# Expert stage of a hybrid encoder block: gate and up products issued as halves of both, and the next tile's rows turned in one place

## The chip, the core and the metric

The program runs on one core of a Trainium2 chip. The metric is the device time of one execution in microseconds (us). TensorE (PE in the profile) multiplies and turns, ScalarE (ACT) and VectorE (DVE) evict and split, GpSimd (POOL) gathers rows and adds results back with indirect DMAs, SyncE (SP) issues the weight loads.

## The reference, cut to what matters

The block projects 2048 tokens of width 1024, runs two attention mixers, merges them, and ends with a mixture of experts. Each token goes to 2 of 32 experts. The change touches this last part alone:

```python
order = jnp.argsort(eid)
tok = order // TOP_K
sizes = jnp.bincount(eid, length=N_EXPERTS).astype(jnp.int32)
xs = xt[tok]
hgu = lax.ragged_dot(xs, w_gate_up, sizes)
g, u = jnp.split(hgu, 2, axis=-1)
ys = lax.ragged_dot(jax.nn.silu(g) * u, w_down, sizes)
ys = ys * wts.reshape(-1)[order][:, None].astype(ys.dtype)
out = jnp.zeros((t, dm), ys.dtype).at[tok].add(ys)
```

`w_gate_up` is 32 x 1024 x 1024 (columns 0 to 511 gate, 512 to 1023 up), `w_down` is 32 x 512 x 1024, all float32.

## The kernel before, in words

Stages follow each other: projection, differential attention, window attention, merge and router, routing tables, experts (`expert_phase`, L2033 to L2340), final normalization. The change is in `expert_phase`.

**Precision.** Every float32 operand of a product is split into a rounded high part (ACT writes it as float32r) and the rest (DVE subtracts). A product is three matmuls: high x high, low x high, high x low. The stationary operand is the activation (128 x 128), the moving one the weight row slice.

**Tiles.** The routing stage sorts the tokens by expert and pads each expert to whole tiles of 128 tokens; `bounds` holds the first tile of each expert, which the engines read into registers (L2073 to L2077). For these inputs there are 49 tiles for 32 experts. PE runs a loop over experts and in it one over the expert's tiles (L2200 to L2217). ACT, DVE and POOL write out an expert's first tile and loop over its further ones.

**A tile on PE.** `gate_or_up` (L2168 to L2183) is called for gate with 512 columns into `p_gate` (8 slices k of the depth, 3 matmuls each, 24 in all), then for the two halves of up with 256 columns into `p_up0` and `p_up1` (24 matmuls each). In the middle of the second half of up, PE turns the first half of `h` (`turn_h(g, 0)`). Then it turns the first half of the next tile's gathered rows `xg` into `px` (`turn_x(g + 1, 0)`, 4 transposes of 128 columns, L2209), multiplies with `w_down` by 4 slices of the depth (`down`, 6 matmuls of 512 columns each, L2185 to L2195), turns the second half of `h` after the first slice (L2213) and the second half of the rows before the last (L2216). `px` has one bank of 512 columns, so the second half may be turned only when DVE has read the first (the wait on `x_lo`, L2155).

**A tile on ACT** (`tile`, L2237 to L2248): Silu of the 512 gate columns into `act_g`; in the first tile of an expert the high parts of slices 0 to 2 of the next expert's weights (`high`, L2221); the high part of the first half of the turned `h` (`hh`); slice 3; the second half of `hh`; the high part of the first half of the next rows (`high_x`, L2233). The second `high_x` follows in the next tile's or expert's code (L2255, L2274, L2279), and so does `result` (L2260), which evicts `py` times the token weights into `yo`.

**A tile on DVE** (`tile`, L2295 to L2317): waits for the Silu, multiplies `act_g` with each half of up as it comes (L2296 to L2298), and subtracts for the low parts of the next expert's early slices, of `h` (`low_h`, L2300) and of the rows (`low_x`, L2290).

**Weights.** An expert's 12 slices (8 of gate and up, 4 of down, 512 KB each) are loaded into `raw` by SP, each as soon as DVE has made the low part of the same slice for the expert before (L2090 to L2096). ACT and DVE make high and low parts: slices 0 to 3 have two places each, so they are made during the expert's first tile (`EARLY = 4`); slices 4 to 7 wait for the last tile's up products, slices 8 to 11 for its down products (L2225 to L2230).

**Rows.** POOL waits until both halves of a tile's rows are turned (L2122, L2128), gathers the next tile's rows, then waits for `yo` and adds the result of the tile before to `acc` (L2109 to L2117).

Of the kernel before, what the change touches and what calls it, by code (L numbers as in the profile page):

```python
# [21 lines left out]
P = 128  # L22
SEQ = 2048
D = 1024
# [2008 lines left out]
def expert_phase(nc, ident, x1, idx, weight, bounds, raw, load_raw, acc):  # L2033
# [6 lines left out]
    EARLY = 4  # L2040
    LATE_X = 6
    KF = FF // P
    NS = KD + KF
# [3 lines left out]
    with Phase(nc, "e") as ph:  # L2047
# [18 lines left out]
        picked, gathered, x_turned, x_hi, x_lo = (ph.sem(n) for n in ("picked", "gathered", "x_turned", "x_hi", "x_lo"))  # L2066
        gate_done, up_done, silu_done, h_done, h_turned, h_hi, h_lo = (
            ph.sem(n) for n in ("gate_done", "up_done", "silu_done", "h_done", "h_turned", "h_hi", "h_lo"))
        down_done, y_out, added, picked_out = ph.sem("down_done"), ph.sem("y_out"), ph.sem("added"), ph.sem("picked_out")
# [79 lines left out]
        def _(pe):  # L2149
            pe.sem_inc(up_done, 1)  # L2150
            pe.sem_inc(down_done, 1)

            def turn_x(g, half):

                pe.wait_ge(x_lo, 2 * g + half + 1)  # L2155
                for c in range(0, HX, P):
                    at = half * HX + c
                    last = nc.tensor.transpose(px[:, c:c + P], xg[:, at:at + P], ident[:])
                last.then_inc(x_turned, 1)
# [40 lines left out]
            with pe.Fori(0, NE) as e:  # L2200
                b0, b1 = tiles(pe, e)
                with pe.Fori(b0, b1) as g:

                    gate_or_up(g, e, p_gate, slice(0, FF), gate_done)
                    for p in range(PIECES):
                        gate_or_up(g, e, p_up[p], slice(FF + p * HP, FF + (p + 1) * HP), up_done)

                    pe.wait_ge(gathered, 16 * (g + 2))
                    turn_x(g + 1, 0)  # L2209

                    pe.wait_ge(y_out, g + 1)
                    down(g, e, 0)
                    turn_h(g, 1)  # L2213
                    down(g, e, 1)
                    down(g, e, 2)
                    turn_x(g + 1, 1)  # L2216
                    down(g, e, 3).then_inc(down_done, 1)  # L2217

        @block.scalar
        def _(act):  # L2220
            def high(e, b0, slices):  # L2221
                for s in slices:
                    if not (isinstance(e, int) and e == 0):
                        act.wait_ge(raw_in[s], 16 * e)
                    if s >= EARLY:  # L2225

                        if s < KD:
                            act.wait_ge(up_done, PIECES * b0 + 1)
                        else:
                            act.wait_ge(down_done, b0 + 1)  # L2230
                    nc.scalar.activation(wh[:, slot(e, s), :], raw[:, s:s + 1, :], ACT.Copy).then_inc(w_hi, 1)  # L2231

            def high_x(g, half):  # L2233
                act.wait_ge(x_turned, 2 * g + half + 1)
                nc.scalar.activation(xh[:, half * HX:(half + 1) * HX], px[:], ACT.Copy).then_inc(x_hi, 1)

            def tile(g, early_of=None):  # L2237
                act.wait_ge(gate_done, g + 1)
                nc.scalar.activation(act_g[:], p_gate[:], ACT.Silu).then_inc(silu_done, 1)
                if early_of is not None:  # L2240

                    high(early_of, None, range(EARLY - 1))
                for p in range(PIECES):
                    act.wait_ge(h_turned, PIECES * g + p + 1)
                    nc.scalar.activation(hh[:, piece(p)], phh[p][:, 0:HP], ACT.Copy).then_inc(h_hi, 1)
                    if early_of is not None and p == 0:
                        high(early_of, None, range(EARLY - 1, EARLY))
                high_x(g + 1, 0)  # L2248

            def expert(e, last):  # L2250
                b0, b1 = tiles(act, e)
                tile(b0, None if last else e + 1)
                with act.If(b0 + 1 < b1):
                    with act.Fori(b0 + 1, b1) as g:
                        high_x(g, 1)  # L2255
                        result(g - 1)
                        tile(g)
                return b1
# [12 lines left out]
            with act.Fori(0, NE - 1) as e:  # L2271
                b1 = expert(e, False)
                high(e + 1, b1, range(EARLY, LATE_X))
                high_x(b1, 1)  # L2274
                high(e + 1, b1, range(LATE_X, KD))
                result(b1 - 1)
                high(e + 1, b1, range(KD, NS))
            b1 = expert(NE - 1, True)
            high_x(b1, 1)  # L2279
            result(b1 - 1)  # L2280

        @block.vector
        def _(dve):
            dve.sem_inc(x_lo, 1)

# [4 lines left out]
            def low_x(g, half):  # L2290
                dve.wait_ge(x_hi, 2 * g + half + 1)
                at = slice(half * HX, (half + 1) * HX)
                nc.vector.tensor_tensor(xl[:, at], px[:], f(xh[:, at]), ALU.subtract).then_inc(x_lo, 1)

            def tile(g, early_of=None):  # L2295
                def multiply(p):  # L2296
                    dve.wait_ge(up_done, PIECES * g + p + 2)
                    nc.vector.tensor_tensor(h[:, piece(p)], act_g[:, piece(p)], p_up[p][:, 0:HP], ALU.mult).then_inc(h_done, 1)  # L2298

# [8 lines left out]

                dve.wait_ge(silu_done, g + 1)
                multiply(0)  # L2310
                early(0, 1)
                low_h(0)
                multiply(1)
                early(2)
                low_h(1)
                low_x(g + 1, 0)
                early(3)  # L2317

            def expert(e, last):
                b0, b1 = tiles(dve, e)  # L2320
                tile(b0, None if last else e + 1)
                with dve.If(b0 + 1 < b1):
                    with dve.Fori(b0 + 1, b1) as g:
                        low_x(g, 1)
                        tile(g)
# [7 lines left out]
            with dve.Fori(0, NE - 1) as e:  # L2333
                b1 = expert(e, False)
                for s in range(EARLY, NS):
                    if s == LATE_X:
                        low_x(b1, 1)
                    low(e + 1, s)
            b1 = expert(NE - 1, True)
            low_x(b1, 1)  # L2340

# [163 lines left out]
```

## Time and profile before

| | |
|---|---|
| median of 3 runs | 2822.14 us (2819.76 to 2827.99) |
| the profiled execution | 2831.76 us |
| its span, first to last instruction | 2830.0 us |
| mean granted TensorE clock over the span | 0.955 of full |
| PE busy | 2608.0 us (92%) |
| DVE busy | 1625.0 us (57%) |
| ACT busy | 1190.8 us (42%) |
| experts stage, first gate matmul to the last tile's down products | about 1859.7 to 2758 us |

All stretches and starts below are us from the span's start. A busy figure of PE counts overlapping matmuls once; matmuls are pipelined, so the distance from one start to the next tells what a matmul costs in a stream, not its recorded duration. "issue" as a releaser means that the profile shows nothing the engine waited for. Names carry a stage's letter: `e_px` is `px` of the expert stage, `rw_raw` is `raw`.

### The profile page before, as it was taken

Reading aid. Unit: us, or ns where it says so; the run is one execution under the profiler, and the core shown is the slowest. Engines: PE = TensorE matmul, PEld = TensorE weight load, DVE = VectorE, ACT = ScalarE, POOL = GpSimd, SP = SyncE. Lnnn points to the kernel's source line nnn. Section 1 sums busy time; section 2 is a strip of 40 time slices with the busy share of each in tenths; the row PEclk is TensorE's granted clock in tenths of the full one; section 3 lists DMA queues with packets and bytes.
Section 4 is the critical chain, followed back from the end, with each engine's and each line's share of the span. In section 5 each row is a group of like instructions: output and inputs, shape, how many; then the busy total and the mean of one; then the engine's idle time right before and its main releaser. Section 6 shows DMA issues by size and latency. Waiting matters only on the chain. (4 is left out here: it accounts for less than half of the span.)

```text
span 2830.0 us, 45509 instructions
## 1 busy us (share of the span) xinstructions
PE 2608.0 (92%) x14631; PEld 2248.3 (79%) x14632; DVE 1625.0 (57%) x3059; ACT 1190.8 (42%) x2016; POOL 527.2 (19%) x538
## 2 busy tenths in 40 slices
PE   6999996899999999989799999589999999999990
PEld 5888885788888888889688888378888888888880
DVE  6323332666666666559544443667585577557846
ACT  3111111445444454447211111357585567556746
POOL 0111111101001010035233332012222222222220
PEclk9999998999999999969899999789999999999995
DMA  6344444756575564279433443469787788768946
GB/s 227 121 158 135 143 153 139 226 183 205 166 213 172 190 208 145 102 178 230 156 117 130 134 139 136 149 209 377 235 316 244 229 294 307 235 227 316 381 123 260
DMA packets 261732, 566.40 MB, mean 200 GB/s; under 512 B 27025, under 2 KB 119953, under 8 KB 259585
## 3 DMA queue, kind: packets, MB, share of 16 engines
q1 hardware_dynamic: 170192, 430.50, 44.6%
q0 software_dynamic: 18720, 64.96, 8.8%
q10 hardware_dynamic: 72720, 69.68, 7.4%
q8 instruction: 56, 0.92, 0.1%
q14 instruction: 44, 0.35, 0.0%
HBM read 433.45 MB, written 131.60 MB: 200 GB/s over the span
## 5 line engine op out<-in xcount | busy, mean ns | idle before, releaser
L2288 DVE TENSOR_TENSOR e_wl<-rw_raw,e_wh 128x1024 fp32r<-128x1024 f32 (+1 forms) x384 | 449.4, 1220 | 18.2 <-ACT e_wh L2231 13.8
L2231 ACT ACTIVATE e_wh<-rw_raw 128x1024 fp32r<-128x1024 f32 (+1 forms) x384 | 380.6, 1054 | 6.4 <-PEq L76 6.4
L246 PE MATMUL j_pg<-qkv_w_hi,j_xh 128*128 128x512 f32 (+1 forms) x640 | 243.6, 381 | 9.2 <-DVE qkv_w_lo L416 9.2
L248 PE MATMUL j_pg<-qkv_w_lo,j_xh 128*128 128x512 f32 (+1 forms) x640 | 238.0, 372 | 0.0
L247 PE MATMUL j_pg<-qkv_w_hi,j_xl 128*128 128x512 f32 (+1 forms) x640 | 237.3, 371 | 0.0
L2180 PE MATMUL e_p_up<-e_wh,e_xh 128*128 128x256 f32 (+1 forms) x784 | 225.5, 288 | 0.0
L2182 PE MATMUL e_p_up<-e_wl,e_xh 128*128 128x256 f32 (+1 forms) x784 | 221.7, 283 | 0.0
L2181 PE MATMUL e_p_up<-e_wh,e_xl 128*128 128x256 f32 (+1 forms) x784 | 221.7, 283 | 0.0
L1136 PE MATMUL b_pg<-b_g_wh,b_g_xh 128*128 128x512 f32 x512 | 209.0, 408 | 0.7 <-DVE b_g_out L1323 0.7
L1193 ACT ACTIVATE b_th<-b_t 128x512 fp32r<-128x512 f32 (+3 forms) x160 | 85.4, 534 | 285.6 <-PE b_t L1121 276.8
L1136 PE MATMUL b_pg<-b_g_wl,b_g_xh 128*128 128x512 f32 x512 | 204.8, 400 | 0.0
L1136 PE MATMUL b_pg<-b_g_wh,b_g_xl 128*128 128x512 f32 x512 | 203.5, 397 | 0.0
L1267 DVE TENSOR_SCALAR_CACHE_REDUCE b_sc<-b_s 128x512 f32<-128x512 f32 (+3 forms) x320 | 179.2, 605 | 30.4 <-PE b_s L1108 18.6
L2192 PE MATMUL e_py<-e_wh,e_hh 128*128 128x512 f32 x392 | 166.8, 425 | 0.4
L1308 DVE TENSOR_TENSOR b_tl<-b_t,b_th 128x512 fp32r<-128x512 f32 (+3 forms) x160 | 97.6, 610 | 119.8 <-ACT b_th L1193 119.8
L445 DVE TENSOR_TENSOR j_by_cos<-j_pg,qkv_cos 128x512 f32<-128x512 f32 x64 | 37.7, 589 | 216.4 <-DMA v_lo<-j_staged 145.8
L2180 PE MATMUL e_p_gate<-e_wh,e_xh 128*128 (+1 forms) x392 | 156.8, 400 | 1.3 <-issue 1.3
L1186 ACT ACTIVATE b_sc<-b_sc,b_nb 128x128 f32<-128x128 f32 (+15 forms) x128 | 153.1, 1197 | 6.8 <-DVE b_nb L1278 6.8
L2194 PE MATMUL e_py<-e_wl,e_hh 128*128 128x512 f32 x392 | 154.5, 394 | 0.0
L2193 PE MATMUL e_py<-e_wh,e_hl 128*128 128x512 f32 x392 | 153.6, 392 | 0.0
L2182 PE MATMUL e_p_gate<-e_wl,e_xh 128*128 (+1 forms) x392 | 153.4, 391 | 0.0
L2181 PE MATMUL e_p_gate<-e_wh,e_xl 128*128 (+1 forms) x392 | 153.4, 391 | 0.0
(350 smaller groups left out, 6634.8 us busy)
## 6 DMA issues: line engine op xcount, KB each, us to landing
rw_raw<-w_gate_up SPq DMA_DIRECT2D x256, 512.0 KB, 7.3
rw_raw<-w_down SPq DMA_DIRECT2D x128, 512.0 KB, 9.5
b_g_xh<-xt_hi SPq DMA_DIRECT2D x64, 512.0 KB
b_g_xl<-xt_lo SPq DMA_DIRECT2D x64, 512.0 KB
gates<-b_g_out ACTq DMA_DIRECT2D x64, 256.0 KB, 5.2
m_gt<-gates SPq DMA_DIRECT2D x16, 1024.0 KB, 8.3
qk_hi<-j_staged ACTq DMA_DIRECT2D x16, 832.0 KB, 4.5
qk_lo<-j_staged ACTq DMA_DIRECT2D x16, 832.0 KB, 6.9
```

Of the source, the lines that this page charges most:

```text
L246: nc.tensor.matmul(out, xh[:, u, ks], w_hi[:, k, cs], start=(k == 0), stop=False)
L247: nc.tensor.matmul(out, xl[:, u, ks], w_hi[:, k, cs], start=False, stop=False)
L248: last = nc.tensor.matmul(out, xh[:, u, ks], w_lo[:, k, cs], start=False, stop=(k == KD - 1))
L1136: last = nc.tensor.matmul(pg[:], x_side, w_side, start=(q == 0), stop=(q == PASSES - 1))
L1267: nc.vector.tensor_scalar(sc[u][:, m, ks], bank[n % 4][:, 0:ks.stop - ks.start], 1.0, NEG, ALU.mult, ALU.max, accum_out=mx[:, u, m, g:g + ...
L2180: nc.tensor.matmul(out[:, 0:js.stop - js.start], xh[:, at], hi, start=(k == 0), stop=False)
L2181: nc.tensor.matmul(out[:, 0:js.stop - js.start], xl[:, at], hi, start=False, stop=False)
L2182: last = nc.tensor.matmul(out[:, 0:js.stop - js.start], xh[:, at], lo, start=False, stop=(k == KD - 1))
L2192: nc.tensor.matmul(py[:, js], hh[:, at], wh[:, n, js], start=(k == 0), stop=False)
L2194: last = nc.tensor.matmul(py[:, js], hh[:, at], wl[:, n, js], start=False, stop=(k == KF - 1))
L2231: nc.scalar.activation(wh[:, slot(e, s), :], raw[:, s:s + 1, :], ACT.Copy).then_inc(w_hi, 1)
L2288: nc.vector.tensor_tensor(wl[:, slot(e, s), :], raw[:, s:s + 1, :], f(wh[:, slot(e, s), :]), ALU.subtract).then_inc(w_lo, 1)
```

## The change

- Gate and up are no longer separate products. Piece p (of two) is columns 256 p to 256 p + 255 of gate and the same of up: one matmul of 512 columns, whose moving operand is two runs of 256 columns that lie 512 apart in the weight slice. Piece p goes to its own bank `p_gu[p]`, gate in its first half and up in its second. 48 matmuls of 512 columns take the place of 24 of 512 and 48 of 256.
- `turn_h(g, 0)` stands before slice 6 of the second piece (before: before slice 4 of the second half of up).
- Silu is done by halves of 256 columns, one after each piece; the second stands behind the early slice 3 on ACT. DVE multiplies a half as soon as its Silu is done.
- `px` has two banks. Both halves of the next rows are turned together, ahead of the down products; ACT's two `high_x` stand before the second half of `hh`, DVE's two `low_x` before the second `low_h`. The places in the next tile's and the next expert's code are gone. The first slice of the first piece waits for the first half of the rows, slice 4 for the second.
- On DVE, early slice 2 comes before the second multiplication.

```diff
+    TURN_AT = 3 * KD // 4
...
-        p_gate, p_up = ph.ps("p_gate", [P, FF]), [ph.ps(f"p_up{p}", [P, BANK]) for p in range(PIECES)]
-        py, px = ph.ps("py", [P, D]), ph.ps("px", [P, HX])
+        p_gu = [ph.ps(f"p_gu{p}", [P, 2, HP]) for p in range(PIECES)]
+        py, px = ph.ps("py", [P, D]), ph.ps("px", [P, D])
...
-            def gate_or_up(g, e, out, js, done):
+            def gate_and_up(g, e, p):
+
                 for k in range(KD):
-                    if out is p_gate:
+                    if p == 0:
                         if k % (KD // 2) == 0:
 
-                            pe.wait_ge(x_lo, 2 * g + 2 + 2 * k // KD)
+                            pe.wait_ge(x_lo, 2 * g + 3 + 2 * k // KD)
                         wait_low(pe, e, k)
-                    if out is p_up[1] and k == KD // 2:
+                    elif k == TURN_AT:
 
                         turn_h(g, 0)
                     at = slice(k * P, (k + 1) * P)
-                    hi, lo = wh[:, slot(e, k), js], wl[:, slot(e, k), js]
-                    nc.tensor.matmul(out[:, 0:js.stop - js.start], xh[:, at], hi, start=(k == 0), stop=False)
-                    nc.tensor.matmul(out[:, 0:js.stop - js.start], xl[:, at], hi, start=False, stop=False)
-                    last = nc.tensor.matmul(out[:, 0:js.stop - js.start], xh[:, at], lo, start=False, stop=(k == KD - 1))
-                last.then_inc(done, 1)
+                    hi, lo = (w[:, slot(e, k), :].rearrange("p a (b n) -> p (a b) n", b=2)[:, :, piece(p)] for w in (wh, wl))
+                    nc.tensor.matmul(p_gu[p][:], xh[:, at], hi, start=(k == 0), stop=False)
+                    nc.tensor.matmul(p_gu[p][:], xl[:, at], hi, start=False, stop=False)
+                    last = nc.tensor.matmul(p_gu[p][:], xh[:, at], lo, start=False, stop=(k == KD - 1))
+                last.then_inc(gu_done, 1)
...
-                    gate_or_up(g, e, p_gate, slice(0, FF), gate_done)
                     for p in range(PIECES):
-                        gate_or_up(g, e, p_up[p], slice(FF + p * HP, FF + (p + 1) * HP), up_done)
+                        gate_and_up(g, e, p)
 
                     pe.wait_ge(gathered, 16 * (g + 2))
                     turn_x(g + 1, 0)
+                    turn_x(g + 1, 1)
 
                     pe.wait_ge(y_out, g + 1)
                     down(g, e, 0)
                     turn_h(g, 1)
                     down(g, e, 1)
                     down(g, e, 2)
-                    turn_x(g + 1, 1)
                     down(g, e, 3).then_inc(down_done, 1)
...
             def tile(g, early_of=None):
-                act.wait_ge(gate_done, g + 1)
-                nc.scalar.activation(act_g[:], p_gate[:], ACT.Silu).then_inc(silu_done, 1)
-                if early_of is not None:
-
-                    high(early_of, None, range(EARLY - 1))
-                for p in range(PIECES):
+                def silu(p):
+                    act.wait_ge(gu_done, PIECES * g + p + 2)
+                    nc.scalar.activation(act_g[:, piece(p)], p_gu[p][:, 0, :], ACT.Silu).then_inc(silu_done, 1)
+
+                def high_h(p):
                     act.wait_ge(h_turned, PIECES * g + p + 1)
                     nc.scalar.activation(hh[:, piece(p)], phh[p][:, 0:HP], ACT.Copy).then_inc(h_hi, 1)
-                    if early_of is not None and p == 0:
-                        high(early_of, None, range(EARLY - 1, EARLY))
+
+                def early(*slices):
+                    if early_of is not None:
+                        high(early_of, None, slices)
+
+                silu(0)
+                early(0, 1, 2)
+                high_h(0)
+                early(3)
+                silu(1)
                 high_x(g + 1, 0)
+                high_x(g + 1, 1)
+                high_h(1)
...
-            dve.sem_inc(x_lo, 1)
+            dve.sem_inc(x_lo, 2)
...
             def tile(g, early_of=None):
                 def multiply(p):
-                    dve.wait_ge(up_done, PIECES * g + p + 2)
-                    nc.vector.tensor_tensor(h[:, piece(p)], act_g[:, piece(p)], p_up[p][:, 0:HP], ALU.mult).then_inc(h_done, 1)
+                    dve.wait_ge(silu_done, PIECES * g + p + 1)
+                    nc.vector.tensor_tensor(h[:, piece(p)], act_g[:, piece(p)], p_gu[p][:, 1, :], ALU.mult).then_inc(h_done, 1)
...
-                dve.wait_ge(silu_done, g + 1)
                 multiply(0)
                 early(0, 1)
                 low_h(0)
+                early(2)
                 multiply(1)
-                early(2)
+                low_x(g + 1, 0)
+                low_x(g + 1, 1)
                 low_h(1)
-                low_x(g + 1, 0)
                 early(3)
```

## Rows read from the trace of the kernel before

**Rows 1.** Groups of instructions of 1800 to 2830, counts and mean ns of one

```profile
L2239 ACT ACTIVATE e_act_g<-e_p_gate 128x512 f32<-128x512 f32 x49 | 29.4, 599 | 72.2 <-PE e_p_gate L2182 71.8
```

**Rows 2.** Busy time by stretch: PE, PEld, DVE, ACT, POOL, then PEclk, DMA share, GB/s

```profile
1859.00:2750.00 891.00, 889.87 (x5247) 776.05 (x5248) 575.82 (x668) 563.05 (x699) 198.09 (x193) 1.00 0.80 274
...
2099.58:2117.99 18.41, 18.41 (x109) 15.94 (x109) 16.50 (x19) 15.99 (x20) 4.30 (x4) 1.00 1.03 385
...
2136.42:2154.49 18.07, 18.07 (x110) 15.79 (x108) 5.07 (x9) 6.08 (x9) 3.63 (x4) 1.00 0.51 170
```

**Rows 3.** Waits of 1855 to 2750: us in total, times, longest

```profile
PEld e_py L2192 <- issue: 7.1, 30, 0.3
```

**Rows 4.** Timeline of PE, an expert's first tile: start, us, what

```profile
2099.58 0.50 PE L2180 MATMUL e_p_gate<-e_wh,e_xh 128*128 x1
...
2105.13 0.28 PE L2180 MATMUL e_p_up<-e_wh,e_xh 128*128 x1
...
2109.44 0.38 PE L2165 MATMUL e_phh<-ident,e_h 128*128 128x128 f32 x2
2109.58 0.36 PE L2180 MATMUL e_p_up<-e_wh,e_xh 128*128 128x256 f32 x1
...
2111.10 0.60 PE L2158 MATMUL e_px<-ident,e_xg 128*128 128x128 f32 x4
2111.70 0.49 PE L2192 MATMUL e_py<-e_wh,e_hh 128*128 128x512 f32 x1
...
2113.18 0.38 PE L2165 MATMUL e_phh<-ident,e_h 128*128 128x128 f32 x2
2113.32 0.48 PE L2192 MATMUL e_py<-e_wh,e_hh 128*128 128x512 f32 x1
...
2116.16 0.60 PE L2158 MATMUL e_px<-ident,e_xg 128*128 128x128 f32 x4
2116.52 0.48 PE L2192 MATMUL e_py<-e_wh,e_hh 128*128 128x512 f32 x1
```

**Rows 5.** Timeline of PE in an expert's second tile, which starts at 2136.42

```profile
2147.84 0.60 PE L2158 MATMUL e_px<-ident,e_xg 128*128 128x128 f32 x4
2148.20 0.48 PE L2192 MATMUL e_py<-e_wh,e_hh 128*128 128x512 f32 x1
```

**Rows 6.** Timeline of ACT in the tile of rows 4

```profile
2105.68 1.28 ACT L2239 ACT_TABLE_LOAD   x1
2106.98 0.60 ACT L2239 ACTIVATE e_act_g<-e_p_gate 128x512 f32<-128x512 f32 x1
2107.47 2.94 ACT L2231 ACTIVATE e_wh<-rw_raw 128x1024 f32 x3
2110.32 0.37 ACT L2245 ACTIVATE e_hh<-e_phh 128x256 fp32r<-128x256 f32 x1
2110.58 1.06 ACT L2231 ACTIVATE e_wh<-rw_raw 128x1024 f32 x1
2113.60 0.39 ACT L2245 ACTIVATE e_hh<-e_phh 128x256 fp32r<-128x256 f32 x1 [1.97 <-PE e_phh L2165]
```

**Rows 7.** Timeline of DVE in the tile of rows 4

```profile
2108.20 0.42 DVE L2298 TENSOR_TENSOR e_h<-e_act_g,e_p_up 128x256 f32<-128x256 f32 x1 [0.61 <-PE e_p_up L2182]
...
2111.05 0.42 DVE L2302 TENSOR_TENSOR e_hl<-e_phh,e_hh 128x256 fp32r<-128x256 f32 x1
...
2114.02 0.42 DVE L2302 TENSOR_TENSOR e_hl<-e_phh,e_hh 128x256 fp32r<-128x256 f32 x1 [1.09 <-ACT e_hh L2245]
2114.51 0.69 DVE L2293 TENSOR_TENSOR e_xl<-e_px,e_xh 128x512 fp32r<-128x512 f32 x1
```

**Rows 8.** Landing of weight loads issued in 2062.74 to 2081.17, then 2117.99 to 2136.42

```profile
DMA to landing us min/median/max: 7.5/9.5/9.8
...
DMA to landing us min/median/max: 11.2/11.4/11.6
```

**Rows 9.** Timeline of PE ahead of the first tile

```profile
1857.36 1.11 PE L2158 MATMUL e_px<-ident,e_xg 128*128 128x128 f32 x4 [1.41 <-DVE e_xl L2293]
```

More of the change, by code:

```diff
@@ L2066, in expert_phase @@
         picked, gathered, x_turned, x_hi, x_lo = (ph.sem(n) for n in ("picked", "gathered", "x_turned", "x_hi", "x_lo"))
-        gate_done, up_done, silu_done, h_done, h_turned, h_hi, h_lo = (
-            ph.sem(n) for n in ("gate_done", "up_done", "silu_done", "h_done", "h_turned", "h_hi", "h_lo"))
+        gu_done, silu_done, h_done, h_turned, h_hi, h_lo = (
+            ph.sem(n) for n in ("gu_done", "silu_done", "h_done", "h_turned", "h_hi", "h_lo"))
         down_done, y_out, added, picked_out = ph.sem("down_done"), ph.sem("y_out"), ph.sem("added"), ph.sem("picked_out")
@@ L2149, in _ @@
         def _(pe):
-            pe.sem_inc(up_done, 1)
+            pe.sem_inc(gu_done, 1)
             pe.sem_inc(down_done, 1)
@@ L2155, in turn_x @@
                 pe.wait_ge(x_lo, 2 * g + half + 1)
-                for c in range(0, HX, P):
-                    at = half * HX + c
-                    last = nc.tensor.transpose(px[:, c:c + P], xg[:, at:at + P], ident[:])
+                for at in range(half * HX, (half + 1) * HX, P):
+                    last = nc.tensor.transpose(px[:, at:at + P], xg[:, at:at + P], ident[:])
                 last.then_inc(x_turned, 1)
@@ L2227, in high @@
                         if s < KD:
-                            act.wait_ge(up_done, PIECES * b0 + 1)
+                            act.wait_ge(gu_done, PIECES * b0 + 1)
                         else:
@@ L2234, in high_x @@
                 act.wait_ge(x_turned, 2 * g + half + 1)
-                nc.scalar.activation(xh[:, half * HX:(half + 1) * HX], px[:], ACT.Copy).then_inc(x_hi, 1)
+                nc.scalar.activation(xh[:, half * HX:(half + 1) * HX], px[:, half * HX:(half + 1) * HX], ACT.Copy).then_inc(x_hi, 1)
             def tile(g, early_of=None):
-                act.wait_ge(gate_done, g + 1)
-                nc.scalar.activation(act_g[:], p_gate[:], ACT.Silu).then_inc(silu_done, 1)
-                if early_of is not None:
-                    high(early_of, None, range(EARLY - 1))
-                for p in range(PIECES):
+                def silu(p):
+                    act.wait_ge(gu_done, PIECES * g + p + 2)
+                    nc.scalar.activation(act_g[:, piece(p)], p_gu[p][:, 0, :], ACT.Silu).then_inc(silu_done, 1)
+                def high_h(p):
                     act.wait_ge(h_turned, PIECES * g + p + 1)
                     nc.scalar.activation(hh[:, piece(p)], phh[p][:, 0:HP], ACT.Copy).then_inc(h_hi, 1)
-                    if early_of is not None and p == 0:
-                        high(early_of, None, range(EARLY - 1, EARLY))
+                def early(*slices):
[6 more added lines that the diff above has]
+                silu(1)
                 high_x(g + 1, 0)
+                high_x(g + 1, 1)
+                high_h(1)
             def expert(e, last):
@@ L2254, in expert @@
                     with act.Fori(b0 + 1, b1) as g:
-                        high_x(g, 1)
                         result(g - 1)
@@ L2272, in _ @@
                 b1 = expert(e, False)
-                high(e + 1, b1, range(EARLY, LATE_X))
-                high_x(b1, 1)
-                high(e + 1, b1, range(LATE_X, KD))
+                high(e + 1, b1, range(EARLY, KD))
                 result(b1 - 1)
@@ L2278, in _ @@
             b1 = expert(NE - 1, True)
-            high_x(b1, 1)
             result(b1 - 1)
@@ L2292, in low_x @@
                 at = slice(half * HX, (half + 1) * HX)
-                nc.vector.tensor_tensor(xl[:, at], px[:], f(xh[:, at]), ALU.subtract).then_inc(x_lo, 1)
+                nc.vector.tensor_tensor(xl[:, at], px[:, at], f(xh[:, at]), ALU.subtract).then_inc(x_lo, 1)
             def tile(g, early_of=None):
                 def multiply(p):
-                    dve.wait_ge(up_done, PIECES * g + p + 2)
-                    nc.vector.tensor_tensor(h[:, piece(p)], act_g[:, piece(p)], p_up[p][:, 0:HP], ALU.mult).then_inc(h_done, 1)
+                    dve.wait_ge(silu_done, PIECES * g + p + 1)
+                    nc.vector.tensor_tensor(h[:, piece(p)], act_g[:, piece(p)], p_gu[p][:, 1, :], ALU.mult).then_inc(h_done, 1)
                 def low_h(p):
@@ L2323, in expert @@
                     with dve.Fori(b0 + 1, b1) as g:
-                        low_x(g, 1)
                         tile(g)
@@ L2335, in _ @@
                 for s in range(EARLY, NS):
-                    if s == LATE_X:
-                        low_x(b1, 1)
                     low(e + 1, s)
-            b1 = expert(NE - 1, True)
-            low_x(b1, 1)
+            expert(NE - 1, True)
 def final_phase(nc, acc, ln_g, ln_b, out):
```

## Prediction, made before the changed kernel was built or run

> **What bounds the kernel now.** I read the busy time by stretch first, with one stretch for the whole stage: PE is busy 889.87 of 891 us at full granted clock (1.00, the 2.4 GHz level), DVE 575.82, ACT 563.05 [rows 2]. The stage is TensorE's. Then the waits: the only one on PE that repeats is before the first `down` product, 7.1 us in 30 times [rows 3]. Then PE's timeline, tile by tile. There are 49 tiles [rows 1] of two kinds. An expert's further tiles take 18.07 us, an expert's first tile 18.41 [rows 2], and the difference sits mostly in one place: from the first turn of the rows to the first `down` product it is 0.60 us in a first tile [rows 4] and 0.36 in a further one [rows 5]. The wait's releaser is called issue, so I look for it on DVE: `low_h(0)` runs from 2111.05 for 0.42, to 2111.47, and PE goes on at 2111.70 [rows 4, 7]. The product waits for the low part of the first half of `h`, 0.24 us a time; 30 x 0.24 = 7.2 agrees with the 7.1. It is late since DVE could multiply only at 2108.20, when the first half of up was done, and then had two early slices to subtract.
>
> **Part 1, fewer matmuls for the same columns.** 36 matmuls of 256 columns take 2109.44 - 2105.13 = 4.31 us, 0.1197 each. For 512 columns I take two stretches of `down`: 6 matmuls behind four turns take 2113.18 - 2111.70 = 1.48, 12 behind two turns 2116.16 - 2113.32 = 2.84; the 6 more cost 1.36, 0.2267 each, and restarting behind turns costs 1.48 - 1.36 = 0.12 [rows 4]. Two of 256 columns cost 0.2394, one of 512 0.2267: 0.0127 less. A tile has 24 such pairs, so it gains 0.305 us. Restarting behind `turn_h(0)` goes from 0.08 (12 matmuls in 2111.10 - 2109.58 = 1.52, against 12 x 0.1197 = 1.44) to 0.12: 0.04 lost.
>
> No matmul of the trace has a moving operand in two runs, so its cost is bounded from both sides: 0.2267 as for one run of 512 (below nothing is excluded, since the same columns must be streamed), and 2 x 0.1197 = 0.2394 if each run costs what a matmul of its own does. I take 0.2267: 512 columns in one instruction is the nearer row, and a run is 1 KB long.
>
> What a matmul costs beyond its columns is 2 x 0.1197 - 0.2267 = 0.0127 us by the rows. The Trainium skill (TensorE: Matmul & The Clock Gate, the wait-not-56-ns section of Part 1 and Back-to-back issue gap) has a warm matmul cost its columns at 2.4 GHz plus about 2.5 ns. By that the pairs would give 24 x 2.5 ns = 0.06 us a tile in place of 0.31. The trace disagrees with it for these float32r streams; the sum goes by the rows.
>
> **Part 2, the rows turned in one place.** Four turns take 0.36, two 0.14 [rows 4, 5], so two more cost 0.22 and eight about 0.80. Before: 0.36 + 0.36 and a second restart of 0.12; after: 0.80. Gain 0.04, which cancels the loss of part 1. Their waits are long met: `px` halves are read in the tile before. POOL's gather starts some 4 us earlier in the tile, behind the earlier turns; it queues ahead of the same `add_rows` and its bytes are the same, and PE asks for them a tile later. `y_out` comes at the tile's start and is asked for 12 us into it.
>
> So each tile loses 0.305 us: 49 x 0.305 = **15.0 us**.
>
> **Part 3, the wait of first tiles.** After the change (offsets from the tile's start; before in brackets): first piece done 5.55 (2105.13 - 2099.58). On ACT the table load is at 6.10, Silu of 256 columns at 7.40 taking 0.37 as `hh` does (0.60), three slices from about 7.7 (7.89), `hh(0)` from 10.5 to 10.9 (10.74) [rows 6]. DVE multiplies behind the Silu and its own backlog at 8.1 (8.62); the two low slices end near 11.0, and `low_h(0)`, which before ran 11.47 to 11.89, ends at 11.4. PE needs it at 5.55 + (24 x 0.2267 + 0.14 + 0.12) + 0.80 = 12.05, later than its end plus the 0.23 it takes to release PE [rows 4, 7]. The wait goes: **7.1 us** [rows 3].
>
> What is late next is the chain behind the second piece, now longer by a Silu. The piece is done at 11.25; ACT is held by slice 3 (10.8 to 11.8), so Silu(1) runs to 12.2, DVE ends slice 2 about 12.6 and multiplies until 13.05. PE turns that half behind the first `down` slice, at 12.05 + 1.48 = 13.53: 0.3 to spare after the release. `hh(1)` comes 0.42 behind that turn and `low_h(1)` another 0.42 + 0.42 later, as at 2113.18, 2113.60, 2114.02 [rows 4, 6, 7]; so 14.79, plus 0.23 for the release 15.02, and PE asks for it at 13.53 + 0.14 + 1.48 = 15.15. The two `high_x` (12.2 to 13.3) and `low_x` (13.1 to 14.4, two of 0.69) [rows 7] fit between, but with little left: 0.1 us.
>
> **The rest.** The second Silu adds about 0.25 us of ACT, the added waits on ACT hold only copies that are not yet due, and ACT and DVE have 2 us of idle in an 18.41 us tile (15.99 and 16.50 busy) [rows 2]: nothing, for as long as that slack lasts. Ahead of the first tile the second half of the rows waits 1.41 us for `low_x` [rows 9]; with two banks it does not. Bounds 0 and 1.4 (the engine runs at half clock there, recorded at 1.11 for four turns, and part of what is gained early is spent at that clock); I take **1.0**.
>
> **Sum.** 15.0 + 7.1 + 1.0 = 23.1 us. The profiled execution took 2831.76 and would take 2808.7. It stands 9.6 above the median of the runs, 2822.14, so the median becomes **2799 us** (-0.8%). A first tile would take 18.41 - 0.305 - 0.24 = 17.87, a further one 17.76.
>
> **Rivals.**
> - *The wait stays, or moves* to `turn_h(1)` or to the third `down` slice, whose margins are 0.1 to 0.3 us. About 0.24 in each of 30 first tiles, 7.1 us: 2806. For: the thin margins; against: the work before them ends earlier in every step.
> - *A matmul's fixed cost is small*, so the merge gives back little. As a mechanism here, the surplus of the 256-column streams would have to lie elsewhere than in the instruction. 24 x 0.0025 x 49 = 2.9 in place of 15.0: 2811. Against: the two cadences of rows 4. This is the page's rule above.
> - *A run costs like a matmul* (the other bound): 48 x 0.0127 x 49 = 29.9 more: 2829. The gate columns, one run before, become two. For: no row excludes it; against: nothing is nearer to it than the plain 512 rows.
> - *The weight loads become the bound*, the rival on the slower side with a point of decision. In experts of one tile the 16 DMA engines show a share of 1.03 [rows 2], and from the first to the last of four such experts the median landing grows from 9.5 to 11.4 us [rows 8]: 0.63 an expert, so an expert's loads need about 18.41 + 0.63 = 19.05 us. At 17.87 it grows by 1.2, to 9.5 + 3 x 1.2 = 13.1. It decides once landing passes about 15 us, what is left of a tile when ACT must have slice 0 again (about 2.7 lie between its read and the next load). Four in a row is the longest I find, and an expert's further tiles (share 0.51) empty the queue. Were all 31 experts ahead of the last bound to 19.05: 31 x 1.18 = 37 us: 2836.
>
> **Numbers.** A measurement of this kernel tells about 0.3% (8.5 us) from no change. Forecast 0.66, wait stays 0.13, small fixed cost 0.06, run cost 0.07, loads 0.05, something between these that leaves it within 0.3% 0.03. Faster takes the first two and most of the third (2811 lies 11 below): 0.83; same: 0.05; slower: the run cost and the loads, 0.12. Range: 2790 (the median itself moved by 8 us over three runs, and the first-tile wait could leave more behind it than 0.24) to 2812, which takes in the wait and the small fixed cost; 0.15 is left out above.
>
> **What would show it.** PE's starts in the two pieces 0.227 apart (0.239: run cost); no gate or up stream of 0.12; tiles 17.87 and 17.76 apart; no wait row on `e_py`, or one on the third slice; the landing of weight loads at 12 to 13 us at the end of four experts, and no wait of `e_wh` on `rw_raw`; the granted clock at 1.00. I am wrong if the cadence is not 0.227, or if first tiles stay more than 0.2 us above further ones.

## Result and profile after

The changed kernel took 2802.35 us in the median of 6 runs (2796.89 to 2809.25), the kernel before in the same session 2827.88 (2819.76 to 2836.09); the ratio is 0.9915, with a 95% interval of 0.9899 to 0.9931. That is 24 us less, 20 to 29 by the interval; the forecast was 23.1 us less. 2802 lies in the range given. The profiled execution took 2799.30 (before: 2831.76). That is 32.5 less, and not all of it is the change's, as the account of the sum below shows.

The stage by stretch, from the first matmul of the second tile to that of the last (47 tiles; the very first tile runs in part at half clock, and its length varies by a microsecond from execution to execution). Columns as in [rows 2], where PEld is TensorE's loading of stationary operands; the second and the third line are a first tile and a further one:

```profile
1872.98:2706.99 834.01, 834.01 (x3949) 690.35 (x3948) 551.24 (x645) 559.24 (x723) 163.42 (x188) 1.00 0.83 284
2085.91:2103.64 17.73, 17.73 (x85) 14.69 (x85) 16.55 (x19) 16.41 (x21) 3.78 (x4) 1.00 1.03 384
2121.36:2139.09 17.73, 17.73 (x85) 14.69 (x84) 5.55 (x9) 7.30 (x11) 2.97 (x4) 1.00 0.71 235
```

The same stretch of the kernel before:

```profile
1879.90:2739.81 859.91, 859.52 (x5078) 749.27 (x5076) 553.02 (x645) 543.16 (x675) 192.54 (x188) 1.00 0.80 275
```

859.91 to 834.01: 25.9 us from 47 tiles. A first tile and a further one are now equally long, where they were 18.41 and 18.07 [rows 2]. PE's granted clock is 1.00 in both.

PE in that first tile (start, us, what). It answers to [rows 4]:

```profile
2085.91 0.39 PE L2181 MATMUL e_p_gu<-e_wh,e_xh 128*128 x1
2086.14 0.39 PE L2182 MATMUL e_p_gu<-e_wh,e_xl 128*128 x1
...
2095.43 0.39 PE L2165 MATMUL e_phh<-ident,e_h 128*128 128x128 f32 x2
2095.58 0.48 PE L2181 MATMUL e_p_gu<-e_wh,e_xh 128*128 128x512 f32 x1
...
2097.03 1.03 PE L2158 MATMUL e_px<-ident,e_xg 128*128 128x128 f32 x8
2097.82 0.48 PE L2193 MATMUL e_py<-e_wh,e_hh 128*128 128x512 f32 x1
...
2099.29 0.38 PE L2165 MATMUL e_phh<-ident,e_h 128*128 128x128 f32 x2
2099.42 0.48 PE L2193 MATMUL e_py<-e_wh,e_hh 128*128 128x512 f32 x1
...
2100.90 0.39 PE L2193 MATMUL e_py<-e_wh,e_hh 128*128 128x512 f32 x1
```

42 matmuls whose moving operand is two runs take 2095.43 - 2085.91 = 9.52 us, 0.2267 each: what one run of 512 columns costs in `down`. Eight turns take 0.79. And the wait before `down` [rows 3] is gone. The waits of PE's weight loads of 1850 to 2740, whole:

```profile
PEld e_px L2158 <- DMA e_xg<-x,e_idx_in: 7.5, 1, 7.5
PEld e_p_gu L2181 <- issue: 1.9, 1, 1.9
```

Both stand ahead of the first tile. A second wait, which is not in [rows 3], went too. In the kernel before, the weight loads that open an expert idled some 0.26 us in each of 31 tiles, and the stream there restarts 0.1 us late: the first 24 products take 5.55 us in [rows 4], and 5.44 in the changed kernel (2085.91 to 2091.35). These are 31 of the 32 times of this line of the kernel before (1855 to 2750):

```profile
PEld e_p_gate L2180 <- issue: 9.7, 32, 1.7
```

ACT and DVE in the tile of 2085.91 (answers to [rows 6, 7]):

```profile
2091.31 1.28 ACT L2240 ACT_TABLE_LOAD   x1
2092.61 0.39 ACT L2240 ACTIVATE e_act_g<-e_p_gu 128x256 f32<-128x256 f32 x1
2092.89 2.95 ACT L2231 ACTIVATE e_wh<-rw_raw 128x1024 f32 x3
2095.86 0.39 ACT L2244 ACTIVATE e_hh<-e_phh 128x256 fp32r<-128x256 f32 x1
...
2099.70 0.38 ACT L2244 ACTIVATE e_hh<-e_phh 128x256 fp32r<-128x256 f32 x1 [0.95 <-PE e_phh L2165]
```

```profile
2093.34 0.42 DVE L2303 TENSOR_TENSOR e_h<-e_act_g,e_p_gu 128x256 f32<-128x256 f32 x1 [0.22 <-issue]
2094.18 2.36 DVE L2293 TENSOR_TENSOR e_wl<-rw_raw,e_wh 128x1024 f32 x2 [0.42 <-ACT e_wh L2231]
2096.46 0.42 DVE L2307 TENSOR_TENSOR e_hl<-e_phh,e_hh 128x256 fp32r<-128x256 f32 x1
...
2097.93 0.41 DVE L2303 TENSOR_TENSOR e_h<-e_act_g,e_p_gu 128x256 f32<-128x256 f32 x1
2098.30 1.29 DVE L2298 TENSOR_TENSOR e_xl<-e_px,e_xh 128x512 fp32r<-128x512 f32 x2
2100.12 0.43 DVE L2307 TENSOR_TENSOR e_hl<-e_phh,e_hh 128x256 fp32r<-128x256 f32 x1 [0.54 <-issue]
```

The table load is at 5.40 us of the tile (2091.31 - 2085.91), 0.70 earlier than in [rows 6]; the first `low_h` ends at 10.97, and PE asks for it at 11.91.

### The profile page after: what moved, and what is told of

Read it like the earlier page. It is cut to its first block and busy times, and to the rows that moved or that the text cites. A ratio compares the mean times of both kernels' runs of the same rounds, so it can differ in the third digit from the quotient of the medians.

```text
span 2797.6 us, 42799 instructions
## 1 busy us (share of the span) xinstructions
PE 2576.8 (92%) x13455; PEld 2181.4 (78%) x13456; DVE 1622.0 (58%) x3059; ACT 1206.8 (43%) x2065; POOL 496.4 (18%) x538
## 5 line engine op out<-in xcount | busy, mean ns | idle before, releaser
L2181 PE MATMUL e_p_gu<-e_wh,e_xh 128*128 128x512 f32 (+1 forms) x784 | 310.4, 396 | 1.5 <-DVE e_xl L2298 1.5
L2183 PE MATMUL e_p_gu<-e_wl,e_xh 128*128 128x512 f32 (+1 forms) x784 | 306.2, 391 | 0.0
L2182 PE MATMUL e_p_gu<-e_wh,e_xl 128*128 128x512 f32 (+1 forms) x784 | 305.6, 390 | 0.0
L246 PE MATMUL j_pg<-qkv_w_hi,j_xh 128*128 128x512 f32 (+1 forms) x640 | 243.3, 380 | 10.1 <-DVE qkv_w_lo L416 10.1
L2181 PEld LDWEIGHTS e_p_gu<-e_wh,e_xh 128*128 128x128 f32 x784 | 147.6, 188 | 31.7 <-issue 1.9
L2183 PEld LDWEIGHTS e_p_gu<-e_wl,e_xh 128*128 128x128 f32 x784 | 147.4, 188 | 31.2
L2182 PEld LDWEIGHTS e_p_gu<-e_wh,e_xl 128*128 128x128 f32 x784 | 147.8, 188 | 28.3
L2193 PE MATMUL e_py<-e_wh,e_hh 128*128 128x512 f32 x392 | 161.1, 411 | 0.0
```

The lines of the kernel that those rows point to most:

```text
L246: nc.tensor.matmul(out, xh[:, u, ks], w_hi[:, k, cs], start=(k == 0), stop=False)
L2181: nc.tensor.matmul(p_gu[p][:], xh[:, at], hi, start=(k == 0), stop=False)
L2182: nc.tensor.matmul(p_gu[p][:], xl[:, at], hi, start=False, stop=False)
L2183: last = nc.tensor.matmul(p_gu[p][:], xh[:, at], lo, start=False, stop=(k == KD - 1))
L2193: nc.tensor.matmul(py[:, js], hh[:, at], wh[:, n, js], start=(k == 0), stop=False)
```

## The experiments

All ratios are to the kernel before. Each run's "steady" figure is the stretch of 47 tiles as above, of its one profiled execution: 859.91 before, 834.01 changed.

### What a matmul costs beyond its columns

`pairs_split`: each product of the changed kernel as two of 256 columns.

```diff
-                for k in range(KD):
+                for b, k in [(b, k) for b in range(2) for k in range(KD)]:
...
-                    nc.tensor.matmul(p_gu[p][:], xh[:, at], hi, start=(k == 0), stop=False)
+                    nc.tensor.matmul(p_gu[p][:, b, :], xh[:, at], hi[:, b, :], start=(k == 0), stop=False)
```

> The changed kernel with each product of 512 columns issued as two of 256 (the gate halves of all slices, then the up halves), into the same bank, with all else as in the changed kernel: 96 matmuls of 256 columns a tile for 48 of 512. Theory (each instruction costs 0.0127 us beyond its columns): starts 0.120 apart, 48 x 0.0127 = 0.61 us a tile more, less 0.04 for the cheaper restart behind the turns, 28 us in all, so it gives back the whole gain: ratio to the kernel before about 1.001, tiles about 18.3 us apart. Rival (a matmul costs some 2.5 ns beyond its columns, and the 256-column streams were slow for another reason): 6 us more than the changed kernel, ratio about 0.993.

Measured: ratio 1.0015 (1.0001 to 1.0029). The stretch:

```profile
1870.87:2736.22 865.35, 865.35 (x6206) 812.81 (x6205) 554.90 (x645) 559.20 (x723) 163.39 (x188) 1.00 0.81 273
```

865.35 - 834.01 = 31.3 us; further tiles are 18.33 long, 0.60 more than the 17.73 of the changed kernel, where 0.57 was expected. All of the gain is given back and a little more, since a tile now issues 96 products for gate and up where the kernel before issues 72. 3 us are a wait that the order of this experiment makes: its first sweep passes the 8 slices in 2.9 us and meets slices whose low part is not made yet (weight-load waits in the same stretch):

```profile
PEld e_p_gu L2181 <- DVE e_wl L2293: 2.9, 16, 0.2
```

So the cost is one of the instruction (0.60 / 48 = 0.0125 us each), and not of the gate, of the up or of a run. Each matmul here has a weight load of its own, and both were doubled; which of the two it is that costs, no run separates. The 2.5 ns that the Trainium skill gives for a warm matmul beyond its columns (TensorE: Matmul & The Clock Gate, Back-to-back issue gap) is not what these streams show.

### Which part ends the wait of first tiles

`merge_only`: merged products with the Silu in halves, but rows turned in two places through one bank. An excerpt of its edit against the changed kernel; ACT's and DVE's places for the rows go back with it:

```diff
-        py, px = ph.ps("py", [P, D]), ph.ps("px", [P, D])
+        py, px = ph.ps("py", [P, D]), ph.ps("px", [P, HX])
...
                     turn_x(g + 1, 0)
-                    turn_x(g + 1, 1)
...
                     down(g, e, 2)
+                    turn_x(g + 1, 1)
```

> The merged products alone: rows turned in two places through one bank, as before the change. Theory: the merge gives 0.27 us in each of 49 tiles (13 us), and it is the earlier multiplication that ends the wait of first tiles before the down products (7 us): the low part is ready at 11.2 us of the tile, PE asks at 11.5. Ratio about 0.993; no wait row on e_py. Rival (the wait went because eight turns now stand ahead of the down products): the wait of 0.24 us stays in 30 tiles, ratio about 0.995. Beside this, the matmul that opens a new expert restarted late by 0.10 us before the change and does not after it; if the late turning of the rows is why, 0.10 us in 31 tiles comes back here (first tiles 17.87, further ones 17.77), if not, both kinds are 17.77.

`rows_apart`: the same places, but with two banks.

> The changed kernel with the second turning of the rows, and what ACT and DVE do with them, put back where they were, but with two banks, so that the turning waits for nothing. Theory: the place of the turns is worth 0.04 us a tile for the merged restart and 0.10 us in each of 31 tiles that open an expert: 2 + 3 = 5 us more than the changed kernel, ratio about 0.993, same as the merge alone. Rival (the late start of an expert comes of the wait of the second turning for the low part of the first half, not of its place): first tiles as short as further ones, only 2 us more than the changed kernel, and faster than the merge alone.

Measured: 0.9954 (0.9939 to 0.9970) and 0.9954 (0.9936 to 0.9973), steady 849.22 and 849.15. The theory of `merge_only` was wrong on the wait, and that of `rows_apart` did not reckon with it: it stays in both. Weight-load waits from 1870 to 2740, of the first:

```profile
PEld e_py L2194 <- issue: 8.7, 30, 0.3
PEld e_p_gu L2182 <- issue: 8.0, 31, 0.3
```

and of the second:

```profile
PEld e_py L2193 <- issue: 12.1, 30, 0.4
```

First tiles are 18.22 long in both, further ones 17.77 to 17.82. The merge alone gives what its step said in further tiles (0.27), and in first tiles no more than 0.2. The late start of an expert is gone with two banks although the turns are late, as the rival of `rows_apart` said: it came with the second turning's wait for the low part of the first half, not with its place. (PE comes to the turns of a first tile at 11.15 us of it, in `merge_only` at 11.26. Why a wait that was met a microsecond before holds up the next expert, no view shows.) But the 0.1 us that this gave in each expert went into the other wait, which grew from 0.3 to 0.4: something else sets the length of a first tile.

What that is, ACT's timeline in `merge_only` shows, in the first tile that starts at 2082.23:

```profile
2081.03 0.60 ACT L2236 ACTIVATE e_xh<-e_px 128x512 fp32r<-128x512 f32 x1 [0.45 <-PE e_px L2159]
2081.52 2.00 ACT L2232 ACTIVATE e_wh<-rw_raw 128x1024 fp32r<-128x1024 f32 x2
2083.41 1.11 ACT L2273 ACTIVATE e_yo<-e_py,weight 128x1024 f32<-128x1024 f32 x1
2084.41 3.90 ACT L2232 ACTIVATE e_wh<-rw_raw 128x1024 fp32r<-128x1024 f32 x4
2088.33 1.28 ACT L2241 ACT_TABLE_LOAD   x1
2089.62 0.38 ACT L2241 ACTIVATE e_act_g<-e_p_gu 128x256 f32<-128x256 f32 x1
2089.90 2.94 ACT L2232 ACTIVATE e_wh<-rw_raw 128x1024 f32 x3
2092.75 0.37 ACT L2245 ACTIVATE e_hh<-e_phh 128x256 fp32r<-128x256 f32 x1
```

From the second turning of the rows to the high part of `h` there is no pause. The chain starts when PE has turned the second half, 1.2 us ahead of the tile, and ends 12 us later with the high part that DVE needs for the value PE waits for. Slices 6 and 7 in it wait only for the last tile's products with gate and up, which were done long before; they stand behind the turning for no reason of their own. From this came the next run.

`slices_first`: `rows_apart` with one exchange on ACT.

```diff
-                high(e + 1, b1, range(EARLY, LATE_X))
-                high_x(b1, 1)
-                high(e + 1, b1, range(LATE_X, KD))
+                high(e + 1, b1, range(EARLY, KD))
+                high_x(b1, 1)
                 result(b1 - 1)
```

> The kernel with the second turning put back (two banks), and one exchange on ACT: slices 6 and 7 of the next expert go ahead of the second high_x, which waits for that turning. Theory: the wait of first tiles before the down products is ACT's: from the second turning to the high part of h it runs without a pause (slices 6 and 7, the eviction of the result, slices 8 to 11, the table load, Silu, slices 0 to 2), and a late second turning holds it up by about a microsecond. With the exchange, the wait of 0.4 us in 30 tiles goes although the rows are still turned late: first tiles 17.8, ratio about 0.991, as of the changed kernel. Rival (the wait is the place of eight turns ahead of the down products, PE's own time): unchanged, first tiles 18.2, ratio 0.995.

Measured: 0.9917 (0.9898 to 0.9935), as good as the changed kernel. The stretch, and PE's waits of 1870 to 2740 whole:

```profile
1871.36:2707.49 836.13, 836.01 (x3949) 688.49 (x3948) 547.97 (x644) 548.00 (x722) 172.85 (x188) 1.00 0.82 283
```

```profile
PEld e_py L2193 <- issue: 0.4, 1, 0.4
```

The theory holds. 849.15 - 836.13 = 13.0 us come from the exchange alone. And 836.13 - 834.01 = 2.1 us, 0.045 a tile, is what turning the rows in one place is worth once the wait is gone: the restart of part 2 (0.04).

### Is it ACT in the kernel before, too?

`low_h_sooner`: the kernel before with an exchange on DVE (the edit below). `before_slices_first`: the kernel before with the exchange on ACT, as in `slices_first`.

```diff
-                early(0, 1)
+                early(0)
                 low_h(0)
+                early(1)
                 multiply(1)
```

> The kernel before with one exchange on DVE: the low part of the first half of h ahead of early slice 1. It prices the wait before the down products by itself. Theory: the high part is ready at 11.1 us of a first tile, the low part then ends at 11.6 in place of 11.9, and PE, which asks at 11.9, no longer waits: 30 x 0.24 = 7 us less, ratio 0.9975, first tiles 18.17. Rival: the wait moves on to the second turning of h or to the third down slice, since slices 1 and 2 now stand ahead of the second multiplication in other order: ratio 1.000.

> The kernel before, with the exchange on ACT alone (slices 6 and 7 ahead of the second high_x). Theory: before the merge it is the first multiplication, held until the first half of up is done at 8.4 us of the tile, that sets when DVE gets through two low slices to the low part of h (11.47); ACT earlier by a microsecond changes nothing there. The wait of 0.24 us stays in 30 tiles, ratio 1.000 within 0.0015. Rival (ACT's unbroken chain sets the wait in this kernel too): the wait goes, 7 us, ratio 0.997 or less.

Measured: 0.9966 (0.9952 to 0.9980) and 0.9969 (0.9957 to 0.9980); steady 852.00 and 853.08, so 7.9 and 6.8 us from a wait of 7.1. Either exchange ends it. The second theory was wrong: in this kernel, too, the wait goes when ACT comes earlier. In the kernel before, ACT stands for the second turning and then works without a pause until the table load of [rows 6]; the start of that chain, 1.2 us ahead of the tile of 2099.58:

```profile
2098.38 0.60 ACT L2235 ACTIVATE e_xh<-e_px 128x512 fp32r<-128x512 f32 x1 [0.43 <-PE e_px L2158]
```

DVE shows how this reaches PE. In `before_slices_first`, multiplication and next early slice:

```profile
2093.86 0.42 DVE L2297 TENSOR_TENSOR e_h<-e_act_g,e_p_up 128x256 f32<-128x256 f32 x1 [0.36 <-PE e_p_up L2182]
2094.20 1.22 DVE L2287 TENSOR_TENSOR e_wl<-rw_raw,e_wh 128x1024 f32 x1
```

and in the kernel before (the multiplication at 2108.20 stands in [rows 7]):

```profile
2108.77 1.23 DVE L2288 TENSOR_TENSOR e_wl<-rw_raw,e_wh 128x1024 f32 x1
```

0.34 from start to start against 0.57. The slice came 0.23 us late since ACT made its high part only from 2107.47 to 2108.52, and this is as much as the 0.24 that PE waited. The view prints no idle time there. The other half of what the prediction said stands: the multiplication at 2108.20 did wait 0.61 us for the first half of up [rows 7], and with one slice in place of two behind it the wait goes as well.

### An order that moves the wait

`merge_low_h_sooner`: `merge_only` with `low_h(0)` ahead of early slice 1, but slices 1 and 2 both ahead of the second multiplication. `merge_low_h_then`: the same with slice 2 behind it; DVE's edit of this one, against the changed kernel:

```diff
-                early(0, 1)
+                early(0)
                 low_h(0)
-                early(2)
+                early(1)
                 multiply(1)
+                early(2)
```

> The merged products alone, rows turned in two places, with the exchange on DVE: the low part of the first half of h ahead of early slice 1. Theory: in the merge alone the wait (0.28 us in 30 tiles) has the low part behind two early slices, of which slice 0 waits for ACT; with one slice in front it starts when ACT has the high part, at 10.9 us, ends at 11.3, and PE, which asks at 11.6, does not wait: 8 us less than the merge alone, ratio about 0.992, first tiles 17.9. Rival (the wait is ACT's high part itself): it shortens by less than half, ratio over 0.994.

> The merged products alone with the low part of the first half of h after one early slice, and slice 2 moved behind the second multiplication. The run before this one left two slices ahead of that multiplication behind the low part: DVE came to it at 13.5 us of the tile and PE waited 1.17 us at the second turning of h in 31 tiles. Theory: now the multiplication runs at 12.4, done at 12.8, and PE turns at 13.06 without a wait, so neither wait is left: first tiles 17.9, ratio about 0.992, against 0.9954 of the merge alone. Rival (DVE has too little room for either order, and some wait stays): ratio over 0.994.

Measured: 1.0028 (1.0016 to 1.0041), slower than the kernel before, and 0.9933 (0.9907 to 0.9958). Steady: 869.11 and 840.10. In the first the wait on `e_py` is gone as expected and another, four times as long, has come (waits of 1870 to 2740):

```profile
PEld e_phh L2166 <- DVE e_h L2307: 35.5, 30, 1.2
```

Two slices of 1.13 us ahead of the multiplication start it at 13.53 us of the tile, and PE wants to turn its result at about 13.1. In the second both waits are gone: first tiles 17.91, as expected (the late start of experts stays). One exchange of 1.1 us on an engine with 2 us of idle a tile is worth 29 us (869.11 - 840.10).

### The room of the second chain

`low_h_late`: the changed kernel with `early(3)` ahead of `low_h(1)` on DVE.

> The changed kernel with early slice 3 on DVE ahead of the low part of the second half of h. The prediction gave that chain 0.1 us to spare in a first tile. Theory: slice 3 takes DVE from about 14.1 to 15.3 us of the tile, the low part then comes at 15.7 in place of 14.65, PE asks for it at 15.0, so a wait of about 0.95 us appears on e_py in 30 to 31 first tiles: 29 us, first tiles 18.7, ratio about 1.002. Rival (the chain has more room than the arithmetic says, or the lost time is made good because the tile after starts with ACT and DVE further ahead): under 0.5 us a tile, ratio under 0.997.

Measured: 0.9957 (0.9941 to 0.9974), steady 847.36: 13.4 us more, 0.44 on average in each of 30 first tiles (18.11 to 18.37 long), where 0.95 was expected. The waits of 1867 to 2740, whole:

```profile
PEld e_py L2193 <- DVE e_wl L2293: 17.7, 30, 0.8
PEld e_p_gu L2181 <- issue: 2.9, 16, 0.2
```

The rival's number came, not by its reasons. The expectation let slice 3 start at 14.1; in the changed kernel DVE is through with the rows at 13.7 (2098.30 + 1.29 - 2085.91) and idle for 0.54 until 14.2, so the slice delays the low part by 1.13 - 0.54 = 0.59. The 0.1 us to spare that the prediction gave this chain was right: in the changed kernel the low part ends at 14.64, reaches PE 0.23 later at 14.87, and PE starts the third slice of the depth at 14.99 (2100.90). 0.59 less these 0.12 is 0.47 a tile, against the 0.44 measured.

### The weight loads

`loads_fewer`: it leaves out the loads of `w_down` after the first expert, so that its output is not the reference's; all instructions of PE, ACT and DVE stay. `loads_more`: one more load of 512 KB an expert. The edit of the first, on SP:

```diff
-                for s in range(NS):
+                for s in range(KD):
```

> The changed kernel without the loads of w_down after the first expert (its slices are split again for every expert, from the first expert's data): 8 loads of 512 KB for 12. Theory (loads are hidden at any landing under about 15 us): no difference from the changed kernel, ratio 0.9915 within 0.0015, tiles 17.73 to 17.78, DMA share about 0.75 in experts of one tile. Rival (the saturated DMA engines already cost something, in waits on the gathered rows or in slower access to the memories): 3 us or more faster than the changed kernel.

> The changed kernel with one more load of 512 KB an expert, into a buffer that nobody reads. At 384 GB/s an expert of one tile then needs (7.34 + 0.52) MB / 384 GB/s = 20.5 us of the DMA engines for 17.74 us of PE; the landing grows by 2.7 us an expert, from 6 to about 14 at the end of four, still inside 15. Theory: no difference from the changed kernel by more than 2 us in all. Rival (the loads are at their limit): every expert of one tile is lengthened towards 20.5 us, up to 2.7 us in each of some 14 tiles, and waits on rw_raw appear on ACT: ratio over 1.000.

Measured: 0.9913 (0.9891 to 0.9934) and 0.9928 (0.9906 to 0.9950); steady 834.72 and 840.59. Without a third of the weight loads nothing changes (all traffic of the steady stretch falls from 284 GB/s to 208, the share in a first tile from 1.03 to 0.91 or 0.96, where 0.75 was expected). 7% more costs 6.6 us in the steady stretch, more than the 2 expected, and 5.5 of it in three tiles: each is the last of four first tiles in a row. One of them, and ACT's waits of 1870 to 2740:

```profile
1947.07:1966.87 19.80, 18.56 (x86) 14.49 (x85) 14.88 (x17) 12.95 (x17) 4.17 (x4) 1.00 1.03 387
```

```profile
ACT e_wh L2237 <- DMA rw_raw<-w_down: 3.5, 9, 1.0
ACT e_wh L2237 <- DMA rw_raw<-w_gate_up: 3.1, 4, 1.1
```

The trace has no landings of this run, but in the tile shown ACT starts its second slice of `w_down` at 1950.23, held by a load that SP issued at 1934.39: 15.8 us, so the point from which the loads decide, about 15 us of landing, was near. The expectation had the fourth expert at 14, and it is already past that point. The longest landing found in the same place of the changed kernel is 12.0 (below), about 3 us short.

## Why the prediction was right, and where it was not

**Part 1, the merge: right.** A pair of 256 columns cost 0.2394, the merged product 0.2267, and the moving operand in two runs costs nothing beyond that. The bound of 0.2394 for it, and with it that rival, is out by the 42 products of 9.52 us. `pairs_split` puts the cost back on the instruction. The rival of a small fixed cost is out with it.

**Part 2, the rows in one place: the sum right, its meaning not.** 0.04 a tile for the merged restart was measured as 0.045. What it left out: with a single bank the second turning waits for DVE, and the stream that opens an expert restarts 0.1 us late. It costs 3 us over 31 experts, and its end has no term in the sum. Further tiles came down by 0.33 instead of 0.305, since the two restarts next to turns that remain cost 0.10 in place of 0.12.

**Part 3, the wait: the size right, the cause in part wrong.** The sum took 7.1 us, and 7 to 8 are measured when it is ended by itself. The step that failed is the one that took ACT's table load at 6.10 over from the rows before, with two low slices ending near 11.0 and `low_h(0)` at 11.4. It left out that DVE's slice 0 stands for ACT, and ACT for the second turning of the rows. With the load at 6.10 and the merge in, `low_h(0)` ends at 11.68, not at 11.4 (`merge_only`, `rows_apart`), and the wait outlives the merge. In the changed kernel the earlier turning lets ACT do slices 4 to 7 before the tile ends, the load moves to 5.40, and `low_h(0)` ends at 10.97. The prediction counted the earlier rows at 0.04 us a tile; yet of the 0.68 us that a first tile lost, the merge alone brought 0.2, and the other 0.48 came only with the earlier rows (or, but for 0.04, with the second bank and the exchange of `slices_first`). That the wait stays was the prediction's first rival, for which it named thin margins and not this chain.

That the wait went by this change was in part luck. The earlier rows work on it in two ways: ACT comes sooner, and PE asks later, since eight turns in place of four stand ahead of `down`. By an estimate from these runs the second way alone would have had nothing to spare: 11.68 + 0.23 = 11.91, against 11.91 when PE asks. No run has eight turns there and the table load still at 6.10; `slices_first` shows that the first way is enough.

**The sum.** For the 47 steady tiles it makes 47 x 0.305 + 7.1 = 21.4 us; 25.9 were measured. The rest is the late start of experts (3) and the cheaper restarts (1). Ahead of the first tile the second half of the rows now follows at once: from the first turn to the first product 3.47 us in place of 4.90, 1.4 gained where 1.0 was taken. Of the other 5 us by which the two profiled executions differ, 2.2 lie ahead of the stage, 2.4 are a first gather that landed sooner, and the rest is in the very first tile, part of it at half clock; of the first two no step of the change gives a reason. The medians, which are 24 us apart by their ratio, agree with the rows of the stage.

**The rival on the slower side** did not decide, and `loads_more` bears out its mechanism. Its "four experts of one tile" are three of one tile and the first tile of a fourth. In the same four tiles of the changed kernel (from 2050.43) the trace has two landings at each change of tiles: loads issued at 2067.50, 2085.24 and 2102.97 land in 6.8, 8.0 and 9.3 us, which is the growth of 1.2 that the prediction gave, and loads issued 2.3 us later in 7.0, 10.1 and 12.0, which is more (3.1, then 1.9). They start lower than the 9.5 that the forecast started from, and 12.0 in the fourth tile stands against its 13.1. Two of these, for 2084 to 2086 and for 2102 to 2104.5:

```profile
DMA to landing us min/median/max: 8.0/8.0/8.0
...
DMA to landing us min/median/max: 9.3/9.3/9.3
```

## What to carry to other kernels

When PE waits for a value, follow the chain behind it through the in-order engines to something that has no idle in front of it, since the engine that delivers last may pass on another's lateness (a distance between starts of 0.57 where it is 0.34 elsewhere is such a wait, even where the view prints none). Work that is already due must not stand in an in-order queue behind an operation that waits for a late event: two copies on the wrong side of one cost 13 us here, and an exchange on DVE made without counting what stands ahead of its next product lost 20 (869.11 against 849.22 of `merge_only`). Issue products at the full 512 columns where the layout allows it, also with a moving operand in two runs.

## What the runs showed of the hardware

- A float32r matmul with new weights each time costs 0.0127 us beyond its columns at full granted clock (2 x 0.1197 at 256 columns less 0.2267 at 512), and a moving operand of two 1 KB runs that lie 2 KB apart costs the same as one run (9.52 us for 42).
- Each further turn of 128 columns of float32 in a series costs about 0.11 us (0.14 for two, 0.36 for four, 0.79 for eight), and the stream of 512 columns behind a series loses about 0.1 (0.12 before; 0.09 and 0.11 in the changed kernel's tile, 2095.58 to 2097.03 and 2097.82 to 2099.29 for 6 products of 0.2267 each).
- In tiles whose loads are a whole expert's, the core's 16 DMA engines show a share of 1.03 at 384 to 387 GB/s (2085.91:2103.64 of the changed kernel, 1947.07:1966.87 of `loads_more`). The matmuls beside them keep their pace: without the loads of `w_down` the steady stretch takes 834.72 us against 834.01.
